# Splitting each gathered expert row into a U transfer and a V transfer, in a mixture-of-experts block fused with a sparse-attention block (Trainium2, one core)

## The chip, the cores and the metric

The kernel runs on one core of one Trainium2 chip. The metric is device time in microseconds (us) of one execution; three runs of the kernel before are shown by their median. One further execution was profiled, and every row below comes from that one.

## The reference, cut to what matters

The program computes two transformer blocks over 16 meta tokens and 256 real tokens of 1024 float32 features. The change lies in the feed-forward part of the first block, a retrieval of single-neuron experts. For each token, 8 heads choose 16 experts each out of 16,384, so 128 experts; for each chosen expert a row of U and a row of V, 1024 floats each, are read:

```python
def block(args):
    xt, e, g = args
    act = jax.nn.gelu(jnp.einsum('nkd,nd->nk', expert_u[e], xt), approximate=False)
    return jnp.einsum('nk,nkd->nd', g * act, expert_v[e])
```

The dot product of the token with the U row goes through a GELU and is scaled by the gate; the V rows are summed with these coefficients.

## The kernel before, in words

**Stages.** The kernel runs its stages one after the other. Most of them multiply activations by weights that SyncE streams from memory in 198 blocks of 512 KB through a ring of four buffers (`ring`, L364), each split into a high and a low part by ScalarE (L297) and VectorE (L305) and used by TensorE (L472). Between `w_peer_q` of the first block and the second block's first norm lies the expert stage, and during it the weight stream stands still.

**The expert stage.** 256 real tokens make two groups of 128, one token per partition. There are 8 heads by 2 token groups, 16 chains of 16 experts, so `SLOTS` = 256 slots. A slot is one expert for each of 128 tokens. For slot n:

- GpSimd (POOL) issues one indirect DMA (L424) that gathers 128 rows of `ROW` = 2048 floats. In the table a U row and its V row lie behind each other, so a row is 8 KB and a slot 1 MB. It goes into one of `ROWS` = 8 buffers of `gathered`. From slot 8 on POOL first waits for `row_used`, which says that slot n-8 has left its buffer (L423). At each sixteenth slot it also waits for `experts_chosen` (L421).
- VectorE waits for `row_landed` (L1463) and multiplies the U half with the token, summing (`dot`, L1469). It signals `dotted`. Between the dots it runs one or two steps of the selection of experts for the chain after next (`route_step`, L1391 to L1448).
- ScalarE waits for `dotted` (L1001), makes the GELU (L1002), the coefficient (L1005) and a diagonal matrix of the coefficients in one of `DIAGS` = 4 buffers (L1009), and signals `diag_ready`. Once per chain, for the first 14, it also makes an exponential between two loads of an activation table (L1029, L1031).
- TensorE waits for `diag_ready` (L687) and multiplies the diagonal with the V half in two matmuls of 512 columns (`add_row`, L689), each of which the profile shows as two. The last one signals `row_used`.

All engines take the slots in order. After 128 slots, and again after 256, ScalarE takes the sums (L1018) and TensorE transposes them (L698); VectorE adds them to the residual (L1489, L1512).

**What sets the order around the change.** Each engine's list of instructions is written out by hand, and semaphores alone tie them together. POOL does nothing else in this stage than issue gathers, one behind the other. A wait in front of one gather holds back all gathers behind it.

The lines that the change touches, beside those that the program prints here: the semaphores `row_landed` (L268), the host's table `rows` (L1716), which joins `expert_u` and `expert_v` along the columns, and the call of `build` (L1725).

Of the kernel before, what the change touches and what calls it, by code (L numbers as in the profile page):

```python
# [25 lines left out]
D = 1024  # L26
# [17 lines left out]
ROW = 2 * D  # L44
ROWS = 8
# [58 lines left out]
BANKS = 4  # L104


def build(nc, stream, rows_dram, small_dram, keys_dram, kiwi_dram, x_dram, out_dram):
    with ExitStack() as ctx:
        def sb(name, shape, dt=F32):
            return ctx.enter_context(nc.sbuf_tensor(name, shape, dt))  # L110

        def sem(name):
            return ctx.enter_context(nc.semaphore(name))
# [10 lines left out]
        small = sb("small", [P, SMALL_COLS])  # L124
# [71 lines left out]
        gathered = work[:, 0:ROWS * ROW].rearrange("p (r n) -> p r n", r=ROWS)  # L196
        base = ROWS * ROW
        route = {}
        for name, n in (("qp", PH * REAL), ("sc", CHAINS * 2 * NKEYS), ("v", 2 * TOPK), ("cand", SPREAD),
# [11 lines left out]
        expert = route["expert"].bitcast(U32)  # L211
# [53 lines left out]
        key_scores_ready, key_scores_taken, tops_shifted, tops_exp, experts_chosen, gates_ready = (  # L265
            sem(n) for n in ("key_scores_ready", "key_scores_taken", "tops_shifted", "tops_exp",
                             "experts_chosen", "gates_ready"))
        row_landed = [sem(f"row_landed{i}") for i in range(ROWS)]  # L268
        row_used, dotted, diag_ready, x_turned = (
            sem(n) for n in ("row_used", "dotted", "diag_ready", "x_turned"))  # L270
        y_summed, y_taken, y_turned, y_ready = (
# [61 lines left out]
        def tile_is_taken(eng, g):  # L333
            eng.wait_ge(tile_taken[g % BANKS], g // BANKS + 1)
# [40 lines left out]
        @block.gpsimd  # L375
        def _(pool):
            g = nc.gpsimd
            for tile, value in ((ones[:, :], 1.0), (eps[:, :], EPS), (one["ones_t"], 1.0), (zeros[:, :], 0.0), (ident[:, :], 0.0),
                                (one["tri"], 1.0), (one["rep"], 0.0), (one["bdtri"], 1.0), (one["win"], 0.0),
                                (one["blk64"], 1.0), (one["hide"], 0.0), (one["keep"], 1.0),  # L380
                                (one["bdm"], 1.0), (one["kbd"], 0.0)):
                g.memset(tile, value).then_inc(zeroed, 1)
            pool.wait_ge(zeroed, 14)
            g.iota(iota[:, :], [[1, NKEYS]], base=0, channel_multiplier=0,
                   allow_small_or_imprecise_dtypes=True).then_inc(consts, 1)
            g.affine_select(out=ident[:, :], in_=ident[:, :], compare_op=ALU.not_equal, fill=1.0, base=0,
                            pattern=[[-1, P]], channel_multiplier=1).then_inc(consts, 1)

            g.affine_select(out=one["tri"], in_=one["tri"], compare_op=ALU.is_ge, fill=0.0, base=0,
                            pattern=[[-1, P]], channel_multiplier=1).then_inc(consts, 1)  # L390

            v = one["rep"][0:META, :].rearrange("p (h m) -> p h m", m=META)
            g.affine_select(out=v, in_=v, compare_op=ALU.not_equal, fill=1.0, base=0,
                            pattern=[[0, P // META], [-1, META]], channel_multiplier=1).then_inc(consts, 1)

            g.memset(one["win"][:, P - META:P], 1.0).then_inc(consts, 1)

            for name, fill, off in (("keep", 0.0, 0), ("hide", NEG, -1)):
                for at, n in ((0, 2 * P), (2 * P, P)):
                    v = one[name][:, at:at + n]  # L400
                    g.affine_select(out=v, in_=v, compare_op=ALU.is_ge, fill=fill, base=off,
                                    pattern=[[1, n]], channel_multiplier=-1).then_inc(consts, 1)

            for n, (name, groups, size, inner) in enumerate((("bdtri", 8, META, META), ("blk64", 2, 64, 64),
                                                             ("bdm", 8, META, 64))):
                v = one[name].rearrange("p (g n) -> p g n", g=groups)
                g.affine_select(out=v, in_=v, compare_op=ALU.is_ge, fill=0.0, base=size - 1,
                                pattern=[[size, groups], [0, inner]],
                                channel_multiplier=-1).then_inc(pool_step, 1)
                pool.wait_ge(pool_step, n + 1)  # L410

                g.affine_select(out=v, in_=v, compare_op=ALU.is_ge, fill=0.0, base=0,
                                pattern=[[-size, groups], [-1 if name == "bdtri" else 0, inner]],
                                channel_multiplier=1).then_inc(consts, 1)

            pool.wait_ge(d_ready, 9)
            g.memset(qbd_flat, 0.0).then_inc(qbd_zeroed, 1)

            for n in range(SLOTS):
                if n % TOPK == 0:  # L420
                    pool.wait_ge(experts_chosen, n // TOPK + 1)  # L421
                if n >= ROWS:
                    pool.wait_ge(row_used, n - ROWS + 1)  # L423
                g.indirect_dma_start(  # L424
                    out=gathered[:, n % ROWS, :], out_offset=None, in_=rows_dram,
                    in_offset=bass.IndirectOffsetOnAxis(ap=expert[:, n:n + 1], axis=0)
                ).then_inc(row_landed[n % ROWS], 16)

            pool.wait_ge(y_ready, 1)
            g.memset(two["vis"], 0.0).then_inc(pool_step, 1)  # L430
            pool.wait_ge(pool_step, 4)
            g.affine_select(out=two["vis"], in_=two["vis"], compare_op=ALU.is_ge, fill=NEG, base=META,
                            pattern=[[-1, META + P]], channel_multiplier=1).then_inc(vis_ready, 1)

            pool.wait_ge(sigmoid_ready, 1)
            for n in range(C):
                tile_is_taken(pool, TILE0["w_conv_out_2"] + n)
                g.tensor_tensor(yco[:, n, :], yco[:, n, :], feat2[:, GB + n, META:],  # L438
                                ALU.mult).then_inc(conv_gated, 1)
# [6 lines left out]
        def _(pe):  # L446
# [168 lines left out]
            for i in range(SUBS):  # L615
                for j in range(2):
                    n = 2 * i + j
# [66 lines left out]
            def add_row(n):  # L684

                t, k = n // (SLOTS // 2), n % (SLOTS // 2)
                pe.wait_ge(diag_ready, n + 1)  # L687
                for j in range(2):
                    last = mm(ps[:, Y_BANK[t] + j, :], diag[:, n % DIAGS, :],  # L689
                              gathered[:, n % ROWS, D + 512 * j:D + 512 * j + 512],  # L690
                              start=k == 0, stop=k == SLOTS // 2 - 1)
                last.then_inc(row_used, 1)
# [10 lines left out]
            for n in range(SLOTS):  # L703
                add_row(n)
                if n == SLOTS // 2 + 4:
                    turn_sums(0, y_turned)
# [42 lines left out]
            for n in range(16):  # L749
# [9 lines left out]
                rows = slice(64 * (h % 2), 64 * (h % 2) + 64)  # L759
# [406 lines left out]
        def _(dve):  # L1166
            v = nc.vector
# [72 lines left out]
            for h in range(8):  # L1240
                rows = slice(64 * (h % 2), 64 * (h % 2) + 64)
                i = v.tensor_copy(kbd[rows, h // 2, META * h:META * h + META], feat[rows, 4 + h // 2, 0:META])
# [71 lines left out]
            for e in range(2):  # L1314
                rows = slice(64 * e, 64 * e + 64)
# [4 lines left out]
            for n in range(2 * SUBS):  # L1320
                i, j = n // 2, n % 2
# [10 lines left out]
            for j in range(2):  # L1332
                for cols, bank, at in ((slice(0, 2 * P), 4 + j, 0), (slice(2 * P, W), 6, 256 * j)):
                    n = cols.stop - cols.start
# [9 lines left out]
            for h in range(4):  # L1344
                i = stt(mix[:, 4 + h, :], ps[:, h // 2, 256 * (h % 2):256 * (h % 2) + 256],
                        small[:, at + h:at + h + 1], sil[:, h, :], ALU.mult, ALU.mult)
# [113 lines left out]
            def dot(n):  # L1460

                t = n // (SLOTS // 2)
                dve.wait_ge(row_landed[n % ROWS], 16 * (n // ROWS + 1))  # L1463
                if n % (SLOTS // 2) == 0:
                    dve.wait_ge(x_turned, t + 1)
                if n >= 2:
                    dve.wait_ge(dotted, n - 1)
                bank = (6, 0)[t]
                v.tensor_tensor_reduce(  # L1469
                    R["product"][:, D * (n % 2):D * (n % 2) + D], gathered[:, n % ROWS, 0:D],  # L1470
                    ps[:, bank:bank + 2, :].rearrange("p b n -> p (b n)"), 1.0, 0.0, ALU.mult, ALU.add,
                    R["dot"][:, n:n + 1]).then_inc(dotted, 1)
# [56 lines left out]
            for t in range(2):  # L1529
                seen = META + P * (t + 1)  # L1530
                for h in range(IDX_HEADS):
                    n = 8 * t + h
# [3 lines left out]
                    out = score[:, t, 0:seen] if h == 0 else rel[:, n % 2, 0:seen]  # L1536
# [25 lines left out]
            u = feat2[:, CU:CU + 8, :]  # L1562
            for c in range(C):
# [10 lines left out]
                i = tt(yc[:, c, :], yc[:, c, :], feat2[:, CB + c, META:], ALU.mult)  # L1574
# [36 lines left out]
            for n in range(8):  # L1611
                ahead(FIRST["w_attn_out_2"] + n)
                g = TILE0["w_attn_out_2"] + n
# [6 lines left out]
                i = tt(ya[:, n, :], yc[:, n, :], yco[:, n, :], ALU.add)  # L1620
# [7 lines left out]
            with dve.Fori(0, FF // 2) as i:  # L1628
                for k in range(RING):
                    ahead(b0 + k, i)  # L1630
                    if k > 1:
                        g = g0 + k
# [96 lines left out]
```

## Time and profile before

| what | value |
|---|---|
| median of 3 runs | 1484.89 us (1483.54 to 1484.93) |
| profiled execution, its own time | 1484.9 us |
| its span, from the first to the last instruction | 1482.9 us |
| outside the span | 2.0 us |
| mean granted TensorE clock | 0.959 of full speed |
| busy: TensorE, VectorE, ScalarE, GpSimd | 85%, 60%, 43%, 18% of the span |
| the chain that ended last, by engine | TensorE 54%, DMA 32% (gathers alone 31%), VectorE 5%, ScalarE 4%, issue 4% |
| gathers: queue, packets, bytes | software_dynamic, 36,864 packets, 268.45 MB |

How to read it: a busy share is an average over stages with different limits. The profile also cuts the span into 40 slices of 37.07 us; the expert stage fills the slices 8 to 24. "DMA" there is the mean busy share of the core's 16 DMA engines and "GB/s" what they moved. The chain that ended last is followed back from the last instruction through what released each step. "Idle before" is how long an engine stood still in front of an instruction, and the name behind the arrow is what ended that wait.

### The profile page before, as it was taken

What the parts mean: (1) busy time and instruction counts of PE and PEld (TensorE: products, weight loads), DVE (VectorE), ACT (ScalarE), POOL (GpSimd) and SP (SyncE); (2) the same over time, 40 slices, a digit from 0 to 9 for tenths busy, and PEclk for the clock granted to TensorE, in tenths of its full rate; (3) what the DMA queues carried; (4) which work ended last, traced back from release to release, by engine and by line L of the source; (5) the groups of instructions that cost most, each with busy time, mean ns of one, the idle gap of its engine ahead of it and who ended that gap; (6) DMA issues with size and microseconds to landing.
All of it is one profiled execution on the core that took longest, in us unless ns stands there. A gap on an engine that the chain in (4) does not pass through costs nothing.

```text
span 1482.9 us, 19506 instructions
## 1 busy us (share of the span) xinstructions
PE 1265.6 (85%) x6686; PEld 893.4 (60%) x6686; DVE 882.4 (60%) x1844; ACT 640.3 (43%) x1395; POOL 262.9 (18%) x300
## 2 busy tenths in 40 slices
PE   5999989677778777777787775899999989899996
PEld 5987778222222222222222222899999989899996
DVE  5445256766666666666666545476835556644455
ACT  4464244344444444444344434334434563533443
POOL 3000000433333333333333330000000020000000
PEclk9999588899999999999999998899999999999998
DMA  5420033999999999999999993245544345455551
GB/s 208 156 86 29 0 114 117 415 420 422 421 422 421 421 421 421 422 421 421 421 406 421 421 420 124 86 143 174 171 139 130 111 134 171 139 185 182 174 182 68
DMA packets 66743, 376.72 MB, mean 254 GB/s; under 512 B 7408, under 2 KB 7408, under 8 KB 33904
## 3 DMA queue, kind: packets, MB, share of 16 engines
q0 software_dynamic: 36864, 268.45, 43.6%
q1 hardware_dynamic: 29664, 106.81, 22.0%
q8 instruction: 38, 0.62, 0.2%
q10 hardware_dynamic: 144, 0.56, 0.1%
q14 instruction: 33, 0.27, 0.0%
HBM read 374.74 MB, written 1.05 MB: 253 GB/s over the span
## 4 chain that ended last, share of the span: by engine, by line
PE 54%; DMA 32%; DVE 5%; ACT 4%; issue 4%; DVEq 0%; SPq 0%; ACTq 0%
PE ps L472 32%; DMA work<-in_rows,work 31%; PE ps L689 6%; PE ps L723 4%; PE ps L507 1%; PE ps L510 1%; PE ps L513 1%; ACT work L1009 1%; PE ps L621 1%; DVE work L1197 1%; DVE work L1469 1%; ACT work L1005 1%; DVE work L1183 1%; DVE work L1202 1%; PE ps L625 1%
## 5 line engine op out<-in xcount | busy, mean ns | idle before, releaser
L689 PE MATMUL ps<-work 128*128 128x512 f32 x1024 | 507.4, 624 | 143.9 <-ACT work L1009 143.6
L689 PEld LDWEIGHTS ps<-work 128*128 128x128 f32 x1024 | 178.4, 192 | 471.5 <-ACT work L1009 324.2
L1469 DVE CUSTOM_DVE_ANT_0 work<-work,ps 128x1024 f32<-128x1024 f32 x256 | 312.7, 1221 | 225.7 <-DMA work<-in_rows,work 225.7
L472 PE MATMUL ps<-x_hi,w_hi 128*128 128x256 f32 (+1 forms) x1280 | 325.8, 295 | 24.2 <-ACT x_hi L315 17.1
L305 DVE TENSOR_TENSOR w_lo<-ring,w_hi 128x1024 fp32r<-128x1024 f32 x198 | 242.6, 1230 | 163.9 <-ACT w_hi L297 162.6
L424 POOL DMA_INDIRECT work<-in_rows,work x256 | 240.1, 938 | 525.7 <-PE ps L689 389.1
L472 PE MATMUL ps<-x_lo,w_hi 128*128 128x256 f32 (+1 forms) x1280 | 316.2, 288 | 0.0
L472 PEld LDWEIGHTS ps<-x_hi,w_hi 128*128 128x128 f32 x1280 | 244.3, 195 | 33.4 <-issue 27.2
L472 PEld LDWEIGHTS ps<-x_lo,w_hi 128*128 128x128 f32 x1280 | 242.4, 193 | 0.3
L297 ACT ACTIVATE w_hi<-ring 128x1024 fp32r<-128x1024 f32 x198 | 204.7, 1052 | 60.3 <-PE ps L723 28.6
L1002 ACT ACTIVATE work<-work 128x1 f32<-128x1 f32 x256 | 51.9, 203 | 357.3 <-DVE work L1469 355.8
L472 PE MATMUL ps<-x_hi,w_lo 128*128 128x256 f32 (+1 forms) x1280 | 186.7, 289 | 0.0
L472 PEld LDWEIGHTS ps<-x_hi,w_lo 128*128 128x128 f32 x1280 | 171.8, 195 | 0.0
L865 ACT ACTIVATE work<-ps 128x272 f32<-128x272 f32 (+2 forms) x96 | 37.7, 393 | 192.2 <-PE ps L472 159.5
L1009 ACT ACTIVATE work<-ident,work 128x128 f32<-128x128 f32 x256 | 102.7, 401 | 8.4
L1005 ACT ACTIVATE work<-work 128x1 f32<-128x1 f32 x256 | 75.4, 294 | 8.3
L438 POOL TENSOR_TENSOR work<-work 128x256 f32<-128x256 f32 x8 | 8.6, 1104 | 294.2 <-ACT work L1113 290.1
L507 PE MATMUL ps<-w_hi,x_hi 128*128 128x256 f32 x192 | 55.2, 287 | 0.0
L513 PE MATMUL ps<-w_hi,x_lo 128*128 128x256 f32 x192 | 53.9, 281 | 0.0
L510 PE MATMUL ps<-w_lo,x_hi 128*128 128x256 f32 x192 | 53.9, 281 | 0.0
L507 PEld LDWEIGHTS ps<-w_hi,x_hi 128*128 128x128 f32 x192 | 36.1, 188 | 1.3 <-issue 0.4
L1140 ACT ACTIVATE work<-ps 128x256 f32<-128x256 f32 x22 | 8.4, 383 | 64.6 <-PE ps L472 64.6
(236 smaller groups left out, 1084.5 us busy)
## 6 DMA issues: line engine op xcount, KB each, us to landing
ring<-in_stream SPq DMA_DIRECT2D x198, 512.0 KB, 3.4
work<-in_rows,work POOLq DMA_INDIRECT x256, 15.3
res<-in_tokens SPq DMA_DIRECT2D x4, 272.0 KB, 3.5
out_dram<-work SPq DMA_DIRECT2D x2, 512.0 KB, 2.8
work<-in_kiwi ACTq DMA_DIRECT2D x1, 544.0 KB, 3.3
work<-in_keys SPq DMA_DIRECT2D x1, 512.0 KB, 9.0
small<-in_small SPq DMA_DIRECT2D x1, 297.0 KB, 5.1
```

The source lines that it names most:

```text
L297: nc.scalar.activation(w_hi[:, k, :], ring[:, k, :], ACT.Copy).then_inc(w_hi_ready, 1)
L305: nc.vector.tensor_tensor(w_lo[:, k, :], ring[:, k, :], w_hi[:, k, :].bitcast(F32), ALU.subtract).then_inc(w_lo_ready, 1)
L424: g.indirect_dma_start(out=gathered[:, n % ROWS, :], out_offset=None, in_=rows_dram, in_offset=bass.IndirectOffsetOnAxis(ap=expert[:, n:n ...
L472: last = mm(out, w[:, k, c * P:(c + 1) * P], x[:, c, :], start=n == 0, stop=n == 3 * C - 1)
L507: i = mm(out, xh[:, c, at:at + P], hi, start=c == 0, stop=False)
L510: i = mm(out, xh[:, c, at:at + P], lo, start=False, stop=False)
L513: last = mm(out, xl[:, c, at:at + P], hi, start=False, stop=c == C - 1)
L689: last = mm(ps[:, Y_BANK[t] + j, :], diag[:, n % DIAGS, :], gathered[:, n % ROWS, D + 512 * j:D + 512 * j + 512], start=k == 0, stop=k == ...
L723: i = mm(ps[:, 4 + m // 2, 256 * (m % 2):256 * (m % 2) + 256], w[:, k, m * P:(m + 1) * P], x, start=False, stop=True, skip_group_check=True)
L1005: link(a(route["coef"][:, n:n + 1], route["gelu"][:, n:n + 1], ACT.Copy, scale=route["gate"][:, n:n + 1]))
L1009: a(diag[:, n % DIAGS, :], ident[:, :], ACT.Copy, scale=route["coef"][:, n:n + 1]).then_inc(diag_ready, 1)
L1469: v.tensor_tensor_reduce(R["product"][:, D * (n % 2):D * (n % 2) + D], gathered[:, n % ROWS, 0:D], ps[:, bank:bank + 2, :].rearrange("p b ...
```

## The change

Each slot's gather becomes two. The table of joined rows becomes two tables, `u` and `v`, of 4 KB rows. For each slot POOL issues a gather of 128 U rows (512 KB) into the first half of the slot's buffer and a gather of 128 V rows into the second half. From slot 8 on the U gather waits for `dotted` of slot n-8 and the V gather for `row_used` of slot n-8. VectorE's dot waits for the U half alone; TensorE gets a wait of its own for the V half. The buffers, their number and all arithmetic stay as they are.

```diff
-        row_landed = [sem(f"row_landed{i}") for i in range(ROWS)]
+        u_landed = [sem(f"u_landed{i}") for i in range(ROWS)]
+        v_landed = [sem(f"v_landed{i}") for i in range(ROWS)]
...
             for n in range(SLOTS):
                 if n % TOPK == 0:
                     pool.wait_ge(experts_chosen, n // TOPK + 1)
+                offset = bass.IndirectOffsetOnAxis(ap=expert[:, n:n + 1], axis=0)
+                if n >= ROWS:
+                    pool.wait_ge(dotted, n - ROWS + 1)
+                g.indirect_dma_start(out=gathered[:, n % ROWS, 0:D], out_offset=None, in_=u_dram,
+                                     in_offset=offset).then_inc(u_landed[n % ROWS], 16)
                 if n >= ROWS:
                     pool.wait_ge(row_used, n - ROWS + 1)
-                g.indirect_dma_start(
-                    out=gathered[:, n % ROWS, :], out_offset=None, in_=rows_dram,
-                    in_offset=bass.IndirectOffsetOnAxis(ap=expert[:, n:n + 1], axis=0)
-                ).then_inc(row_landed[n % ROWS], 16)
+                g.indirect_dma_start(out=gathered[:, n % ROWS, D:ROW], out_offset=None, in_=v_dram,
+                                     in_offset=offset).then_inc(v_landed[n % ROWS], 16)
...
             def add_row(n):
                 t, k = n // (SLOTS // 2), n % (SLOTS // 2)
+                pe.wait_ge(v_landed[n % ROWS], 16 * (n // ROWS + 1))
                 pe.wait_ge(diag_ready, n + 1)
...
             def dot(n):
                 t = n // (SLOTS // 2)
-                dve.wait_ge(row_landed[n % ROWS], 16 * (n // ROWS + 1))
+                dve.wait_ge(u_landed[n % ROWS], 16 * (n // ROWS + 1))
...
-    arrays = {"stream": stream, "rows": np.concatenate([a["expert_u"][0], a["expert_v"][0]], axis=1), "small": np.ascontiguousarray(small),
+    arrays = {"stream": stream, "u": a["expert_u"][0], "v": a["expert_v"][0], "small": np.ascontiguousarray(small),
```

## Rows read from the trace of the kernel before

**Rows 1.** Stretches: busy us (instructions) of each engine, granted clock, DMA share, GB/s.
```profile
core 0: us, PE busy (x) PEld busy (x) DVE busy (x) ACT busy (x) POOL busy (x), PEclk, DMA share, GB/s
8.20:11.70 3.50, 1.25 (x2) 0.50 (x2) 3.36 (x5) 1.96 (x4) 3.43 (x4) 1.00 1.02 416
270.00:570.00 300.00, 238.03 (x481) 84.55 (x480) 199.16 (x543) 127.31 (x386) 112.36 (x120) 0.98 1.01 421
...
745.00:755.00 10.00, 9.86 (x19) 4.31 (x20) 7.46 (x25) 3.68 (x13) 3.57 (x4) 0.83 0.95 369
755.00:895.00 140.00, 109.63 (x223) 37.57 (x222) 80.12 (x185) 56.06 (x176) 51.71 (x56) 1.00 1.01 421
895.00:900.00 5.00, 4.00 (x9) 1.39 (x9) 2.52 (x5) 1.80 (x6) 0.00 (x0) 1.00 0.76 315
902.00:906.00 4.00, 3.33 (x7) 1.35 (x8) 2.38 (x4) 1.03 (x4) 0.00 (x0) 1.00 0.06 27
```

**Rows 2.** Who waited for whom, us 257 to 912: total us, times, longest.
```profile
POOL work L424 <- PE ps L689: 389.1, 246, 5.5
...
DVE work L1469 <- DMA work<-in_rows,work: 225.7, 252, 2.2
```

**Rows 3.** The gathers of L424: duration in ns, and from issue to landing.
```profile
L424 POOL DMA_INDIRECT work<-in_rows,work x256: 933/936/1124, 257.0 to 892.0; - x128
...
DMA to landing us min/median/max: 6.4/15.3/16.3
```

**Rows 4.** DMA in us 8.2 to 11.7, weights and keys, no gather: packets and queue.
```profile
DMA packets 401, 1.45 MB, mean 416 GB/s; under 512 B 46, under 2 KB 46, under 8 KB 401
...
q1 hardware_dynamic: 401, 1.45, 101.9%
```

**Rows 5.** DMA in us 270 to 570, inside the expert stage: packets and queue.
```profile
DMA packets 17349, 126.41 MB, mean 421 GB/s; under 512 B 1923, under 2 KB 1923, under 8 KB 1923
...
q0 software_dynamic: 17335, 126.26, 101.2%
```

**Rows 6.** DMA in us 257 to 912: instruction fetches; on the page, those of the span.
```profile
q8 instruction: 8, 0.13, 0.1%
...
span 1482.9 us, 19506 instructions
...
q8 instruction: 38, 0.62, 0.2%
```

**Rows 7.** POOL in order of time, us 256 to 276: start, duration, idle before.
```profile
256.98 1.12 POOL L424 DMA_INDIRECT work<-in_rows,work  x1 [129.78 <-DVE work L1447]
258.41 0.94 POOL L424 DMA_INDIRECT work<-in_rows,work  x1 [0.30 <-issue]
259.65 0.94 POOL L424 DMA_INDIRECT work<-in_rows,work  x1 [0.31 <-issue]
...
264.62 0.94 POOL L424 DMA_INDIRECT work<-in_rows,work  x1 [0.30 <-issue]
265.87 0.93 POOL L424 DMA_INDIRECT work<-in_rows,work  x1 [0.31 <-issue]
```

**Rows 8.** POOL around two of its gathers with a wait, close together.
```profile
585.78 0.94 POOL L424 DMA_INDIRECT work<-in_rows,work  x1 [3.28 <-PE ps L689]
587.17 0.94 POOL L424 DMA_INDIRECT work<-in_rows,work  x1 [0.46 <-PE ps L689]
```

**Rows 9.** POOL around one of ScalarE's exponentials, us 497 to 514.
```profile
501.06 0.94 POOL L424 DMA_INDIRECT work<-in_rows,work  x1 [2.51 <-PE ps L689]
506.37 0.94 POOL L424 DMA_INDIRECT work<-in_rows,work  x1 [4.38 <-PE ps L689]
```

**Rows 10.** The last slot and what follows it, in order of time.
```profile
907.30 1.22 DVE L1469 CUSTOM_DVE_ANT_0 work<-work,ps 128x1024 f32<-128x1024 f32 x1 [1.23 <-DMA work<-in_rows,work]
...
909.58 1.98 PE L689 MATMUL ps<-work 128*128 128x512 f32 x4 [0.48 <-ACT work L1009]
911.61 1.09 ACT L1018 ACTIVATE work<-ps 128x512 f32<-128x512 f32 x2 [2.07 <-PE ps L689]
```

More of the change, by code:

```diff
@@ L104, with build @@
 BANKS = 4
-def build(nc, stream, rows_dram, small_dram, keys_dram, kiwi_dram, x_dram, out_dram):
+def build(nc, stream, u_dram, v_dram, small_dram, keys_dram, kiwi_dram, x_dram, out_dram):
     with ExitStack() as ctx:
@@ L1724 @@
     out = nc.dram_tensor("out_dram", (P, C * REAL), F32, kind="ExternalOutput").ap()
-    build(nc, dram["stream"], dram["rows"], dram["small"], dram["keys"], dram["kiwi"], dram["tokens"], out)
+    build(nc, dram["stream"], dram["u"], dram["v"], dram["small"], dram["keys"], dram["kiwi"], dram["tokens"], out)
     r = run_bass_kernel_spmd(nc, [{f"in_{k}": v for k, v in arrays.items()}], core_ids=[0])
```

## The prediction

> **What bounds the kernel now.** I began with the table of stretches. From 270 to 570 us and from 755 to 895 us the core's 16 DMA engines are busy all the time (share 1.01) and move 421 GB/s [rows 1]. So the expert stage runs at the pace of its transfers: a slot is 1,048,576 bytes, at 421 GB/s 2.49 us, and 256 slots are 638 us of the 650 us between the first gather and the last dot [rows 7, 10]. The second view, who waited for whom, confirms it from the consumer's side: VectorE waited for gathered rows 252 times out of 256, 225.7 us in all, while POOL waited 389.1 us for TensorE to give buffers back [rows 2]. POOL's wait looks like a lack of buffers, but a gather takes 15.3 us from its issue to its landing and only 6.4 us where nothing is queued ahead of it [rows 3]. Most of a buffer's life is spent in the DMA queue. A buffer that comes free sooner makes that queue longer and moves no byte sooner.
>
> The third view is the end of the stage. From 902 to 906 us the DMA share is 0.06, one engine of sixteen, at 27 GB/s [rows 1]. The others are through at about 899 (0.76 of the 5 us from 895 on). One DMA engine is some 7 us behind the rest, every slot waits for its part, and its work sets the stage's length. Instruction fetches fit as the cause: 8 in this stage, 0.1% of 16 engines over 655 us, so up to 1.3 us each [rows 6].
>
> **The change part by part.** The sum is made against the profiled execution's own time, 1484.9 us (span 1482.9 and 2.0 outside); the median of the runs is the same to 0.1 us. From no change a measurement of this kernel can tell about 0.2%, 3 us.
>
> *The DMA engines.* 128 packets of 8 KB and 16 completion packets per slot become 256 of 4 KB and 32. The trace has no gather of 4 KB rows. The nearest row is the start of the kernel, where 512 KB blocks with 4 KB per partition fill the engines as fully (share 1.02): 416 GB/s, against 421 for the gathers [rows 1]. A slot at 416 GB/s is 2.521 us instead of 2.491, 0.030 us more, times 256 = 7.7 us. The upper bound comes from the time that packets take. At the start 16 engines times 3.5 us times 101.9% is 57.1 us for 355 data packets, 0.161 us each with their completions [rows 4]. In the gathers it is 16 x 300 x 101.2% = 4858 us for 15,412, 0.315 each [rows 5]. Two small ones are 0.006 us longer than one large one; an engine has 8 such pairs per slot, 0.05 us, times 256 = 13 us. The lower bound is nothing: I exclude a gain, as no row shows 4 KB packets faster than the gathers. I take 7.7, since it is a rate of whole transfers at a full load and the upper bound counts the overlap of packets twice.
>
> [...]
>
> *POOL.* 256 more gathers of 0.94 us. Unhindered, issues follow each other in 1.24 us, 0.30 of it between two instructions (259.65 to 265.87, five intervals) [rows 7]. Two per slot are 2.49 us, which is all of a slot's time. Today POOL is busy half of it. 511 intervals from 257.2 put the last V gather at 892.4 us; today's last is issued at 892.0 [rows 3]. So POOL alone doesn't lengthen the stage, and at 2.52 us per slot it keeps 0.03 us spare: cost 0. What it loses is the power to catch up. Around ScalarE's exponential TensorE is late, and POOL stands still for 4.38 us in place of some 1.5 [rows 9]; fourteen chains have that. A lag of 3 us then stays for many slots. It is covered by the queue: 15.3 less 6.4 is 9 us of work ahead of each gather. Once POOL lags, its waits are already met and further stalls pass it by.
>
> *The waits on POOL.* U of slot n waits for `dotted` of n-8, V for `row_used` of n-8. `dotted` comes earlier: the dot starts 2.28 us before TensorE, and TensorE takes 1.98 more [rows 10]. But U of n stands behind V of n-1 in POOL's list, and that waits for `row_used` of n-9. The U half can thus start about one issue (1.24 us) earlier than now, and no more. It lengthens a queue that is already long: 0.
>
> *VectorE and TensorE.* A dot needs only the U half, which the slowest engine delivers half a slot, 1.25 us, before the V half. In the stage this moves the dots forward without making the engine faster. At the end it counts: today 2.28 us lie between the last landing and TensorE's start on it [rows 10]; with U landing 1.25 us earlier 1.03 us are left. Gain 1.25. TensorE's new wait is for a V half that lands within 1.25 us of the U half, while the coefficient takes 2.28: met when it is reached, and TensorE works 2 us of 2.49. At the start the first dot waits for VectorE's routing, not for rows: 0.
>
> *Instruction fetches.* About 256 gathers and 256 waits of TensorE are added to a program that fetches 38 packets for 19,506 instructions, 513 per packet [rows 6]: one more, about 1 us if it hits the slowest engine. I take 1.
>
> Sum: +7.7 - 1.25 + 1 = +7.4, so 1492.3 us.
>
> **The rivals.** *No change to tell.* The 416 of the start is a stretch of 3.5 us only. If the engines are limited by bytes and the small packets cost under 0.012 us per slot (3 us in all), the tail's gain and the cost cancel: 1484.9 - 1.25 + 0 to 3 = 1484 to 1487. Against it: the number of completion packets doubles for certain.
>
> *Faster.* The U half no longer waits for `row_used`, dots run 1.25 us ahead, and the one hole in the transfers, 369 instead of 421 GB/s from 745 to 755 [rows 1], closes. That hole is 10 x (1 - 369/421) = 1.2 us. With the tail's 1.25 it makes 2.5, and with free packets 1482.4 us; over 0.2% needs a little more than the trace holds. This is the other side of my forecast, and it decides only where 4 KB packets cost nothing.
>
> *POOL becomes the bound.* All intervals of 1.24 us are between gathers without a wait. The shortest between two with a wait is 1.39 (585.78 to 587.17), and there TensorE released the second [rows 8]. So an interval with a wait that is already met lies between 1.24 and 1.39. After the last V issue come at least 6.4 less half a slot, 5.2, to the landing, and 2.0 of TensorE. At 1.24 that ends at 899.6, today TensorE ends at 911.6 [rows 10], with my forecast at 919: POOL decides above 1.28 us. At 1.31 the end is 933.8, +22; at 1.39 the last issue is at 967.5 and the end at 974.7, +63, so 1548. Also, up to 16 transfers would be in flight where 8 are now, and nothing shows what POOL does with so many. For it: 512 issues without a margin. Against: 256 gathers of 0.936 us in the median, the longest 1.124 [rows 3], beside a busy VectorE.
>
> *The slow engine falls further behind.* If its lag comes from reading the gathers' descriptors rather than from fetches, twice as many descriptors double the 7 us: 1492.3 + 7 = 1499. [...]
>
> *The change doesn't do what it says.* Separate release of the halves is mostly undone by POOL's fixed order, as worked out above. I hold this for certain, and it is in the forecast.
>
> **How the numbers follow.** The forecast (packets cost 5 to 13 us) has 0.45; the slow engine 0.10; POOL as the bound 0.17; no change 0.20; faster 0.08. Slower by over 0.2% is the first three, 0.72. The time is the forecast's, 1492.3. Its own range is 1488 (5 us for packets) to 1499 (13 us and two fetches). The range reaches down to 1484, the no-change case, and up to 1506, POOL with an interval of 1.31 us. Left out are the faster case and the upper part of POOL's, together under 0.2.
>
> **What would show it.** Right: in the expert stage a DMA share of 1.0 and about 416 GB/s; 512 gathers of 0.94 us; VectorE still waiting for U rows nearly each slot, about 0.6 to 1.2 us; POOL waiting only some tens of us in all; the last gather's landing near 914 us and TensorE's last matmul 3 us behind it. The POOL rival: issues at equal intervals above 1.28 us without waits, landings in 5 to 7 us, DMA share under 0.97. The slow engine: a stretch of 10 us or more at share 0.06 at the end. The forecast is wrong if the rate in the stage is 421 GB/s or more, or if the transfers have gaps while POOL never waits.

## The result, and the profile after

The changed kernel takes 1504.96 us (median of 4 runs, 1504.11 to 1505.45); the kernel before took 1484.91 beside it. The ratio is 1.0136, 95% interval 1.0120 to 1.0152: slower by 20 us. The forecast was 1492.3 with a range up to 1506.0. The direction and the engine were right; the size was 2.7 times the 7.4 us that I had summed. Of the six runs with gathers of 64 rows, further down, four were slow (1888 to 2033 us), so the median of the two others stands there, though the profile is of a slow one.

The profiled execution spans 1502.1 us, 19.2 more than before. First the page: engines, queues and DMA issues of the changed kernel.

```profile
PE 1265.0 (84%) x6686; PEld 896.8 (60%) x6686; DVE 882.7 (59%) x1844; ACT 640.2 (43%) x1395; POOL 503.9 (34%) x556
...
q0 software_dynamic: 73728, 268.47, 44.9%
...
work<-in_u,work POOLq DMA_INDIRECT x256, 16.0
work<-in_v,work POOLq DMA_INDIRECT x256, 16.0
```

The same bytes come in twice the packets (73,728 for 36,864). POOL is busy nearly twice as long (503.9 us for 262.9), VectorE, ScalarE and TensorE as long as before. Then the stretches, which answer to [rows 1]; the columns are busy us (instructions) of each engine, granted clock, DMA share and GB/s.

```profile
8.20:11.70 3.50, 1.25 (x2) 0.50 (x2) 3.36 (x5) 1.82 (x4) 3.43 (x4) 1.00 1.02 411
270.00:570.00 300.00, 231.28 (x470) 83.31 (x469) 194.93 (x530) 124.42 (x377) 225.09 (x240) 0.98 1.03 409
...
745.00:755.00 10.00, 7.58 (x17) 2.71 (x16) 6.15 (x15) 4.92 (x15) 7.25 (x9) 1.00 1.03 410
755.00:895.00 140.00, 106.22 (x217) 37.50 (x216) 81.98 (x197) 55.63 (x172) 101.10 (x108) 0.99 1.03 409
...
915.00:920.00 5.00, 3.83 (x9) 1.35 (x8) 2.44 (x5) 1.80 (x6) 0.00 (x0) 1.00 0.37 150
920.00:925.00 5.00, 3.92 (x9) 1.35 (x8) 2.45 (x5) 1.79 (x6) 0.00 (x0) 1.00 0.08 29
```

The engines are full (1.03) and yet move only 409 GB/s for the whole stage, where they moved 421. A slot is 1,048,576 bytes: 2.564 us in place of 2.491. The difference of 0.073 us times 256 is 18.7 us, nearly all of the loss. Look at the first row too: the stretch on which the forecast's main term stood, the same code in both kernels, reads 411 here and read 416 before.

The waits from 270 to 910 us (total us, times, longest) show who is held up by whom, as [rows 2] did.

```profile
DVE work L1474 <- DMA work<-in_u,work: 234.8, 245, 2.3
...
POOL work L430 <- issue: 69.2, 217, 0.4
POOL work L426 <- issue: 65.0, 213, 0.4
POOL work L430 <- PE ps L694: 23.4, 34, 3.0
```

VectorE still waits for rows at almost every slot. POOL is hardly held up by TensorE any more (23.4 us); what stands between its gathers is the 0.30 us between two instructions. The end of the stage, in order of time, answers to [rows 10]:

```profile
924.37 1.22 DVE L1474 CUSTOM_DVE_ANT_0 work<-work,ps 128x1024 f32<-128x1024 f32 x1 [1.27 <-DMA work<-in_u,work]
...
926.74 1.95 PE L694 MATMUL ps<-work 128*128 128x512 f32 x4 [0.55 <-ACT work L1014]
928.73 1.09 ACT L1023 ACTIVATE work<-ps 128x512 f32<-128x512 f32 x2 [2.14 <-PE ps L694]
```

TensorE ends at 928.7 us against 911.6: 17.1 us later. The remaining 2.1 us of the span lie behind the stage, in code that the change doesn't touch. Stretches of 100 us there, with the whole remainder last; the kernel before:

```profile
911.60:1482.90 571.30, 530.03 (x4146) 513.86 (x4146) 328.54 (x493) 252.54 (x387) 9.15 (x10) 0.96 0.44 143
```

and the changed kernel:

```profile
928.70:1502.10 573.40, 532.15 (x4146) 516.00 (x4146) 328.38 (x493) 252.46 (x387) 9.14 (x10) 0.96 0.43 142
1178.70:1278.70 100.00, 94.01 (x725) 90.14 (x725) 57.06 (x81) 52.02 (x77) 8.62 (x8) 0.98 0.43 139
1278.70:1378.70 100.00, 93.32 (x751) 92.60 (x751) 53.35 (x58) 42.34 (x53) 0.00 (x0) 0.95 0.51 167
```

The same 4146 matmuls take 2.1 us longer. In the second and third rows the granted clock averages 0.98 and 0.95; before, the two stretches at the same distance from the stage's end (1161.6 to 1261.6 and 1261.6 to 1361.6) had 1.00 and 0.97, so TensorE's granted clock was a little lower here. The same remainder, from TensorE's end in the expert stage to the end of the span, took 571 to 575 us in the profiles of all versions below but the one with 64 rows, and 575.3 in one that differs from the kernel before in its last slot alone. So the 2.1 us are within what this part varies by.

### The profile page after: what moved, and what is told of

It is laid out like the page before. It is cut to its first block, busy times and chain, and to the rows that moved or that the text cites. A ratio compares the mean times of both kernels' runs of the same rounds, so it can differ in the third digit from the quotient of the medians.

```text
span 1502.1 us, 20017 instructions
## 1 busy us (share of the span) xinstructions
PE 1265.0 (84%) x6686; PEld 896.8 (60%) x6686; DVE 882.7 (59%) x1844; ACT 640.2 (43%) x1395; POOL 503.9 (34%) x556
## 3 DMA queue, kind: packets, MB, share of 16 engines
q0 software_dynamic: 73728, 268.47, 44.9%
## 4 chain that ended last, share of the span: by engine, by line
PE 51%; DMA 19%; POOL 13%; issue 7%; ACT 5%; DVE 4%; DVEq 0%; SPq 0%; ACTq 0%
PE ps L476 31%; DMA work<-in_u,work 19%; POOL work L430 7%; POOL work L426 6%; PE ps L728 4%; PE ps L694 3%; PE ps L511 1%; PE ps L514 1%; PE ps L517 1%; PE ps L625 1%; DVE work L1202 1%; ACT L1036 1%; ACT L1034 1%; ACT work L1014 1%; DVE work L1188 1%
## 5 line engine op out<-in xcount | busy, mean ns | idle before, releaser
L476 PE MATMUL ps<-x_hi,w_hi 128*128 128x256 f32 (+1 forms) x1280 | 326.4, 296 | 24.2 <-ACT x_hi L316 17.1
L426 POOL DMA_INDIRECT work<-in_u,work x256 | 240.7, 940 | 207.6 <-DVE work L1452 129.7
L430 POOL DMA_INDIRECT work<-in_v,work x256 | 240.3, 939 | 94.1 <-issue 70.8
```

Of the source, the lines that this page charges most:

```text
L426: g.indirect_dma_start(out=gathered[:, n % ROWS, 0:D], out_offset=None, in_=u_dram, in_offset=offset).then_inc(u_landed[n % ROWS], 16)
L430: g.indirect_dma_start(out=gathered[:, n % ROWS, D:ROW], out_offset=None, in_=v_dram, in_offset=offset).then_inc(v_landed[n % ROWS], 16)
L476: last = mm(out, w[:, k, c * P:(c + 1) * P], x[:, c, :], start=n == 0, stop=n == 3 * C - 1)
```

## The experiments

Three theories. *Packets:* the DMA engines pay for each data packet, so 4 KB rows are slower than 8 KB rows whoever issues or waits. *Transfers:* what costs is the second transfer of a slot, with its completion packets, what has to be prepared for it, and its issue. *Release:* the new waits or POOL's full list hold the transfers up. Times are medians; GB/s are those of 270 to 570 us. The figures in square brackets are 95% intervals of the ratio to the kernel before, which ran beside each version.

**Both halves released and awaited together.** The split alone, without the separate release.

```diff
-                    pool.wait_ge(dotted, n - ROWS + 1)
+                    pool.wait_ge(row_used, n - ROWS + 1)
                 g.indirect_dma_start(out=gathered[:, n % ROWS, 0:D], ...)
-                if n >= ROWS:
-                    pool.wait_ge(row_used, n - ROWS + 1)
...
                 dve.wait_ge(u_landed[n % ROWS], 16 * (n // ROWS + 1))
+                dve.wait_ge(v_landed[n % ROWS], 16 * (n // ROWS + 1))
```

> The changed kernel, still with two gathers per slot, but both halves of a buffer are released together (the U gather waits for row_used too, the V gather for nothing of its own) and VectorE waits for both halves before a dot. Packet theory (the DMA engines pay for each packet of 4 KB, whoever waits for what): nothing changes but the end, 1504 to 1507 us, 409 GB/s in the stage. Release theory (the cost lies in the new waits or in POOL being held up between two halves): most of the 20 us come back, 1485 to 1492 us.

Measured: 1505.11 us (1503.78 to 1506.63), ratio to before 1.0134 [1.0114, 1.0154].

```profile
270.00:570.00 300.00, 227.22 (x467) 80.96 (x466) 193.44 (x523) 123.59 (x374) 222.38 (x238) 0.99 1.03 409
```

The release theory falls: with the old rule of release the loss is the same. In the medians of the runs, releasing and awaiting each half by itself neither costs nor brings anything. In the traces it brings the little that was forecast for the end: from the first gather to TensorE's last matmul this version takes 673.7 us (254.7 to 928.4) and the changed kernel 671.9 (256.8 to 928.7).

**Two gathers of 64 rows of 8 KB.** Meant to double the transfers and leave the data packets as they are.

```diff
-                g.indirect_dma_start(
-                    out=gathered[:, n % ROWS, :], out_offset=None, in_=rows_dram,
-                    in_offset=bass.IndirectOffsetOnAxis(ap=expert[:, n:n + 1], axis=0)
-                ).then_inc(row_landed[n % ROWS], 16)
+                for part in range(2):
+                    g.indirect_dma_start(
+                        out=gathered[64 * part:64 * part + 64, n % ROWS, :], out_offset=None, in_=rows_dram,
+                        in_offset=bass.IndirectOffsetOnAxis(ap=expert[0:64, n:n + 1], axis=0)
+                    ).then_inc(half_landed[part][n % ROWS], 16)
...
-                dve.wait_ge(row_landed[n % ROWS], 16 * (n // ROWS + 1))
+                for part in range(2):
+                    dve.wait_ge(half_landed[part][n % ROWS], 16 * (n // ROWS + 1))
```

> The kernel before with two gathers per slot, each of 64 rows of 8 KB, issued and released together. Data packets stay 128 of 8 KB per slot, transfers and completion packets double. The partitions 64 to 127 get the rows of the tokens 0 to 63, so their sums are of other experts. Packet theory, with the 0.072 us per slot spread evenly over 8 more data packets and 1 more completion packet per engine, 0.008 us each: only the completion is left, +2 us, 1487 us, about 419 GB/s. Transfer theory (what costs is a transfer: its issue, its descriptors, its completion): all of the stage's 17 us, 1502 us, 409 GB/s.

Measured: 1857.41 us (1851.61 and 1863.19), ratio 1.2507 [1.2465, 1.2549]. Neither theory had this.

```profile
DMA packets 10360, 67.91 MB, mean 226 GB/s; under 512 B 2073, under 2 KB 2073, under 8 KB 2073
...
q0 software_dynamic: 10354, 67.85, 101.5%
```

The engines are as full as before (101.5% for 101.2%), but a packet of 8 KB takes 16 x 300 x 101.5% / 8281 = 0.588 us, against 0.315 before [rows 5]. Each transfer writes to 64 neighbouring partitions of the 128, and the stage moves 226 GB/s in place of 421. That the number of partitions sets the rate is my estimate from these two rates; no run varied the partitions otherwise. The two gathers of a slot also read the same 64 rows, and no run tells whether that cost something. As a test of transfers against packets it failed, since it changed something larger.

**Rows of 16 KB, one gather for two slots.** The packet theory in the other direction.

```diff
+                if n % 2:
+                    continue
                 if n >= ROWS:
-                    pool.wait_ge(row_used, n - ROWS + 1)
+                    pool.wait_ge(row_used, n - ROWS + 2)
                 g.indirect_dma_start(
-                    out=gathered[:, n % ROWS, :], out_offset=None, in_=rows_dram,
+                    out=work[:, ROW * (n % ROWS):ROW * (n % ROWS + 2)], out_offset=None, in_=rows_dram,
...
-                dve.wait_ge(row_landed[n % ROWS], 16 * (n // ROWS + 1))
+                dve.wait_ge(row_landed[n % ROWS // 2 * 2], 16 * (n // ROWS + 1))
...
-"rows": np.concatenate([a["expert_u"][0], a["expert_v"][0]], axis=1)
+"rows": np.concatenate([a["expert_u"][0], a["expert_v"][0]] * 2, axis=1)
```

> The kernel before with one gather of 128 rows of 16 KB for two slots; both slots compute with the expert of the even one. Per slot and engine 4 data packets of 16 KB in place of 8 of 8 KB, and half a completion. Packet theory with 0.008 us per packet: 4.5 fewer, 0.036 us per slot, -9 us, 1476 us, about 427 GB/s. If the rate is capped by bytes above 8 KB packets: 1484 to 1486 us and 421 GB/s. If releasing buffers in pairs starves the engines: DMA share under 0.98 and a time above 1487 us.

Measured: 1478.12 us (1476.83 to 1480.70), ratio 0.9953 [0.9938, 0.9968], 7 us faster. The page's rates in 40 slices:

```profile
GB/s 209 157 86 30 0 115 107 419 428 422 428 427 406 413 429 427 422 415 428 427 409 428 427 424 126 89 155 171 171 144 128 110 134 171 139 186 180 173 182 65
```

The undisturbed slices of the stage stand at 427 to 429, as foretold; others fall to 406, and so the mean is 423. POOL's longest wait for a pair of buffers between 270 and 570 us is 13.4 us, which makes the release in pairs the likely cause of the falls; it wasn't tested by itself. The three sizes are now in line: a slot takes 2.450 us at 428 GB/s, 2.491 at 421 and 2.564 at 409. That is 0.041 us for 4 more packets per engine, then 0.073 for 8 more: 0.009 to 0.010 us each.

**Half the bytes.** What can POOL do by itself?

```diff
-                g.indirect_dma_start(out=gathered[:, n % ROWS, 0:D], ...)
+                g.indirect_dma_start(out=gathered[:, n % ROWS, 0:D // 2], ...)
...
-                g.indirect_dma_start(out=gathered[:, n % ROWS, D:ROW], ...)
+                g.indirect_dma_start(out=gathered[:, n % ROWS, D:D + D // 2], ...)
```

The tables have rows of 512 floats, the dot reads 512 features and both matmuls read `D:D + 512`.

> The changed kernel with half the bytes of every U and V row: 512 gathers of 128 rows of 2 KB; the dot runs over 512 features and both matmuls use the same 512 columns. The DMA engines need at most 1.4 us per slot, TensorE 1.7, so POOL's issues alone set the pace. If a wait that is already met costs POOL nothing, issues follow each other in 1.24 us also from slot 8 on, 2.49 us per slot, last issue near 893 us, TensorE's end near 899 us, total about 1472 us. If a met wait costs up to 0.15 us (intervals of 1.39 us), 2.79 us per slot and about 1548 us. Only in the first case had the changed kernel's POOL 0.07 us per slot to spare.

Measured: 1476.88 us (1475.70 to 1480.01), ratio 0.9942 [0.9923, 0.9961]. POOL in order of time, and its V gathers:

```profile
299.82 0.95 POOL L426 DMA_INDIRECT work<-in_u,work  x1 [0.30 <-issue]
301.07 0.94 POOL L430 DMA_INDIRECT work<-in_v,work  x1 [0.30 <-issue]
302.32 0.95 POOL L426 DMA_INDIRECT work<-in_u,work  x1 [0.30 <-issue]
```

```profile
L430 POOL DMA_INDIRECT work<-in_v,work x256: 942/946/958, 258.6 to 896.7; - x128
...
DMA to landing us min/median/max: 3.4/3.7/4.5
```

With waits that are already met the interval is 1.25 us, against 1.24 without waits [rows 7]. POOL's own pace is 2.50 us per slot, and here it is the bound: gathers land 3.7 us after their issue, so nothing is queued. The time is 5 us above the 1472 expected, of which the 0.01 us per issue explains most (the last V gather is issued at 896.7 in place of 893), and far below the 1548 of costly waits. At half the bytes the kernel gains no more than 8 us. In the changed kernel POOL had 0.06 us per slot to spare.

**Plain loads from POOL, 8 KB and 4 KB rows.** 128 consecutive rows in place of chosen ones, so the sums are of other experts; the same holds for all versions with plain loads below.

```diff
-                g.indirect_dma_start(
-                    out=gathered[:, n % ROWS, :], out_offset=None, in_=rows_dram,
-                    in_offset=bass.IndirectOffsetOnAxis(ap=expert[:, n:n + 1], axis=0)
-                ).then_inc(row_landed[n % ROWS], 16)
+                g.dma_start(gathered[:, n % ROWS, :], rows_dram[P * (n % 128):P * (n % 128) + P, :]
+                            ).then_inc(row_landed[n % ROWS], 16)
```

The 4 KB version does the same with both transfers of the changed kernel.

> The kernel before, but POOL issues a plain load of 128 consecutive rows of the joined table in place of the gather (other experts, so other sums). Same queue, same 8 KB packets, consecutive addresses. If random rows cost nothing in memory: 421 GB/s and 1483 to 1486 us. If the gathers lose time to scattered rows: up to 427 GB/s, 1475 us.

> The changed kernel with plain loads of 128 consecutive rows of 4 KB, U and V apart, issued by POOL. Packet theory: the rate is that of 4 KB packets whatever the addresses, 409 GB/s, and the time is 17 to 20 us above the kernel with plain loads of 8 KB. If scattered 4 KB rows are what costs: no more than 5 us above it, and 416 GB/s or more. POOL's time per plain load is not known; if it is over 1.28 us, POOL is the bound and the DMA share tells so.

Measured: 1486.35 us (ratio 1.0014 [1.0004, 1.0025]) and 1503.32 us (1.0126 [1.0109, 1.0144]), 17.0 us apart. The 8 KB version:

```profile
270.00:570.00 300.00, 239.01 (x481) 85.05 (x480) 198.50 (x540) 127.65 (x387) 63.82 (x121) 0.98 1.01 421
```

The 4 KB version:

```profile
270.00:570.00 300.00, 228.61 (x469) 81.40 (x467) 193.90 (x530) 124.65 (x378) 123.62 (x234) 0.99 1.03 409
```

These are the rates of the gathers, 421 and 409. Scattered rows cost no rate against consecutive ones, at either size. A plain load also keeps POOL busy for 0.53 us (123.62 / 234) in place of 0.94, so POOL had plenty to spare and the loss was nearly the same.

**The same loads from SyncE's hardware queue.** SyncE's loop over the weight blocks is cut after block 43 and the loads of the 256 slots stand between, with the waits of the kernel before (8 KB) or of the changed one (4 KB).

```diff
-            with sp.Fori(1, BLOCKS // RING) as i:
+            with sp.Fori(1, 11) as i:
...
+            for n in range(SLOTS):
...
+                sp.dma_start(gathered[:, n % ROWS, :], rows_dram[P * (n % 128):P * (n % 128) + P, :]).then_inc(row_landed[n % ROWS], 16)
+            with sp.Fori(11, BLOCKS // RING) as i:
```

> The kernel before with the loads of 128 consecutive 8 KB rows issued by SyncE in its hardware queue, with the same waits; POOL issues none. If the software queue and its descriptors cost nothing: as the plain loads from POOL, 421 GB/s. If they cost: above 421 GB/s and below 1484 us.

> The same with 4 KB rows of U and V apart, by SyncE, with the waits of the changed kernel. It tells what the 416 GB/s at the start of the kernel before was worth, which is this kind of transfer over 3.5 us. If a hardware queue really moves 4 KB packets at 416: 2.52 us per slot, 1490 to 1493 us, 7 to 8 above the 8 KB version, and the rest of the 17 us belongs to the software queue. If 416 was an accident of a short window: 409 to 411 GB/s and 15 to 20 us above the 8 KB version.

Measured: 1483.32 us (ratio 0.9998 [0.9987, 1.0008]) and 1500.51 us (1.0107 [1.0090, 1.0124]), 17.2 us apart, at 421 and at 409 GB/s. The stretch at the start and the one in the stage, of the 4 KB version:

```profile
8.20:11.70 3.50, 1.24 (x2) 0.50 (x2) 3.40 (x4) 1.94 (x4) 3.36 (x5) 1.00 1.02 414
270.00:570.00 300.00, 227.46 (x469) 80.98 (x468) 193.88 (x527) 124.66 (x377) 0.00 (x0) 0.99 1.03 409
```

Both rows are the same queue and the same packet size, once over 3.5 us and once over 300. The short one lies 5 GB/s above the long one. That is no accident of a short window: over the 13 profiles of this study the stretch at the start reads 405 to 420, in the mean 416 and in twelve of them 411 or more, while the 80 stretches of 3.5 us from 270 to 550 us of this version read 403 to 412. The start really moves its 4 KB packets faster than the stage does, and it isn't the queue or the packet size that makes the difference, since both are the same here.

**One transfer of 4 KB runs, and one of two slots.** Transfers and packets pulled apart at last, with plain loads from POOL. The first takes U and V of a slot from two tables in one transfer:

```diff
-                g.dma_start(gathered[:, n % ROWS, :], rows_dram[P * (n % 128):P * (n % 128) + P, :]
+                g.dma_start(gathered[:, n % ROWS, :].rearrange("p (h n) -> p h n", h=2),
+                            uv_dram[:, P * (n % 128):P * (n % 128) + P, :].rearrange("h p n -> p h n")
```

> The kernel with plain loads from POOL, one transfer per slot as before, but of two runs of 4 KB per partition (U and V tables apart): 4 KB packets with one transfer's 16 completion packets and the waits of the kernel before. Packet-size theory (the 0.072 us per slot come with the 4 KB data packets): 409 to 411 GB/s, 1500 to 1504 us. Transfer theory (they come with the second transfer, its completions or its issue): 421 GB/s, 1483 to 1487 us.

The second loads two slots in one transfer, with the waits of the 16 KB rows:

```diff
+                g.dma_start(work[:, ROW * (n % ROWS):ROW * (n % ROWS + 2)].rearrange("p (h n) -> p h n", h=2),
+                            rows_dram[P * (n % 128):P * (n % 128) + 2 * P, :].rearrange("(h p) n -> p h n", h=2)
```

> Plain loads from POOL, one transfer for two slots, of two runs of 8 KB per partition: 8 KB packets, half the transfers and half the completion packets, buffers released in pairs. Packet-size theory: as one transfer per slot, 421 GB/s, 1484 to 1487 us. Transfer theory, by which half a transfer less per slot saves half of 0.072 us: 427 GB/s, 1476 us. Read beside the 16 KB rows, which gave 423 GB/s.

Measured: 1506.32 us (1502.43 to 1507.89, ratio 1.0134 [1.0114, 1.0153]) and 1489.25 us (1485.09 to 1491.18, 1.0028 [1.0015, 1.0040]). DMA of the first, from 270 to 570 us:

```profile
DMA packets 31814, 122.74 MB, mean 409 GB/s; under 512 B 1868, under 2 KB 1868, under 8 KB 31801
```

and of the plain loads with two transfers per slot:

```profile
DMA packets 33686, 122.76 MB, mean 409 GB/s; under 512 B 3743, under 2 KB 3743, under 8 KB 33671
```

The completion packets are halved (1868 for 3743), the data packets are equal, and the rate is 409 in both. The transfer theory falls: the second transfer, its completions and its issue change nothing in the rate. The rates of the second kernel in slices:

```profile
GB/s 208 156 86 29 1 114 133 423 421 422 420 420 407 413 422 421 420 419 412 409 411 422 422 421 124 87 155 171 170 148 120 114 128 163 136 185 182 173 183 68
```

Its good slices are at 421 or 422, not at 427: fewer transfers with the same packets gain nothing. It has falls to 407 and 413 as the 16 KB rows have, and shares with them the one transfer for two slots and the paired release. Both times are some 2 us above the top of what the packet theory had given (1504 and 1487); in both profiles the part behind the stage took 575 us, the upper end of what it takes anywhere.

**The last slot alone split.** The gain at the end by itself.

```diff
+                if n < SLOTS - 1:
                     g.indirect_dma_start(out=gathered[:, n % ROWS, :], ..., in_=rows_dram, ...).then_inc(row_landed[n % ROWS], 16)
+                else:
+                    g.indirect_dma_start(out=gathered[:, n % ROWS, 0:D], ..., in_=u_dram, ...).then_inc(row_landed[n % ROWS], 16)
+                    g.indirect_dma_start(out=gathered[:, n % ROWS, D:ROW], ..., in_=v_dram, ...).then_inc(v_landed, 16)
```

> The kernel before, with the last slot alone split into a U gather and a V gather. The tail term by itself: the last dot starts half a slot earlier, TensorE starts about 1.1 us after the last landing in place of 2.3 and ends near 910.4 us in place of 911.6, total 1483.7 us; in the median of the runs hardly to be told from 1484.9. If the tail's gain was none, TensorE ends at 911.6 us or later.

Measured: 1485.95 us (12 runs, 1482.35 to 1488.07), ratio 1.0003 [0.9993, 1.0014]: no difference.

```profile
904.53 1.22 DVE L1477 CUSTOM_DVE_ANT_0 work<-work,ps 128x1024 f32<-128x1024 f32 x1
...
905.56 3.70 PE L697 MATMUL ps<-work 128*128 128x512 f32 x8 [0.49 <-ACT work L1017]
```

The last dot starts with no wait in front of it, right behind the one before. TensorE then finds two slots together (8 matmuls in one piece) and ends at 909.3, 4.7 us after the start of the last dot, 4.3 before. It ends 2.3 us earlier than before, but its first gather was also 1.3 us earlier (255.7 for 257.0), which leaves 1.0. From the landing of the last V half (issued at 891.7, landed 14.0 us later) to TensorE's end are 3.5 us, where the whole row took 4.3: the split gains 0.8 us there, less than 1.2, since TensorE still has the slot before in hand. Behind the stage this execution loses that again: 575.3 us from 909.3 to its end, against 571.3. No version that computes the same sums is faster than the kernel before; the 16 KB rows are, but two experts that a token chooses don't lie side by side.

## Why the prediction was right or wrong

**What bounds the stage: right.** The DMA engines' share stayed at 1.0 and more, VectorE waited for rows at 251 of 256 slots, and loads from three kinds of issue gave one rate for one packet size: gathers, plain loads from POOL and loads from SyncE moved 421 GB/s in rows of 8 KB and 409 in rows of 4 KB.

**The term for the DMA engines: the step that failed, in its size.** I put +7.7 us, taking the 416 GB/s at the start of the kernel for the rate of 4 KB rows in the stage, and 13 us as the upper bound. It is 409 GB/s, 0.073 us per slot, +18.7. The mechanism was the one named, a price per packet, and the experiments confirm it against both rivals: between 4 and 16 KB the difference comes to 0.009 to 0.010 us per packet of an engine. In every run with full engines a packet is one row, so whether the price belongs to the packet or to the piece of memory that it reads stays open.

What was wrong was the step from one stretch to the other. 416 was not an unlucky reading: it is the mean of that stretch over the 13 profiles. In the changed kernel, 78 of the 80 stretches of 3.5 us from 270 to 550 us read 403 to 412 (the first two 387 and 419). So the start moves the same size of packet some 7 GB/s faster, and that hid 7 of the 12 GB/s that I had to forecast. Neither the queue nor the packet size does it, as the loads from SyncE show; which of the other differences does, what is read, how much is in flight or what the other engines do meanwhile, no run shows. The bound from packet durations came from the same 3.5 us, so it was no second witness: it gave 0.161 us per 4 KB packet, where the changed kernel has 16 x 300 x 102.5% / 29,925 = 0.164, from the two rows of its DMA between 270 and 570 us:

```profile
DMA packets 33681, 122.74 MB, mean 409 GB/s; under 512 B 3741, under 2 KB 3741, under 8 KB 33666
...
q0 software_dynamic: 33666, 122.59, 102.5%
```

With 0.1644 the same working gives (2 x 0.1644 - 0.3152) x 8 = 0.109 us per slot, 28 us in all. Durations do overstate, as I had said, since 18.7 was measured; but by this working the upper bound was 28 and not 13, and the forecast's own range, 1488 to 1499, was too narrow.

**POOL: right.** No cost. Its interval with met waits is 1.25 us, under the 1.28 from which it would decide, and the gathers' landing times tell that it runs ahead: their medians (U, changed kernel) grow from 6.8 us between 270 and 300 us to 14.6 between 450 and 500, and stay at 16.5 to 16.7 after that. That is 0.1 us per slot (7.8 us in some 74 slots) by which the DMA engines fell behind POOL, not the reverse; 0.06 to 0.07 of it is the mean rate (2.564 less 2.50), and the slowest engine's own lag fits as the rest. The loads from SyncE, with no work for POOL at all, gave the same 409 GB/s. That the time landed near the top of a range whose upper end was POOL's is chance, not support for that rival. (An interval of 1.31 us gives 1507 by my own sum, not the 1506 of the range.)

The landings of the U gathers, first from 270 to 300 us, then from 450 to 500:

```profile
DMA to landing us min/median/max: 6.4/6.8/7.2
...
DMA to landing us min/median/max: 13.9/14.6/16.2
```

**The slow engine: the rival fell.** At the end the mean of the engines is through at about 917 (0.37 of the 5 us from 915 on), the last U half lands at 924.3 and the V half at 925.6: 9 us of lag. The kernel before had 907.2 less 899, so 8. That reading the gathers' descriptors causes the lag was the rival's supposition; no row shows such reads. Twice the gathers, in twice the packets (73,728 for 36,864), didn't double it. And with the 8 KB loads in SyncE's hardware queue

```profile
895.00:900.00 5.00, 4.00 (x9) 1.35 (x8) 2.49 (x5) 1.80 (x6) 0.00 (x0) 1.00 0.59 240
```

the mean is through at 898.0 and the last dot starts at 903.9, a lag of 6 us; with the 4 KB loads there it is 7. Most of the lag is there without the gathers. What makes one engine slow stays open.

**The waits: right.** Holding back the separate release left the rate at 409 GB/s and the time within 0.2 us.

**The tail: right in the changed kernel, in the traces.** From the last dot's start to TensorE's is 2.37 us, and the V half lands half a slot, 1.3, after U, so 1.1 us are left of 2.3. From the last landing to TensorE's last matmul are 3.1 us; with both halves awaited together 4.5, and 4.3 in the kernel before. Gain 1.2. The medians of the runs are too coarse to show it (1504.96 and 1505.11). The stage ends 17.1 us later, which is 18.7 less 1.2 within half a microsecond.

**Instruction fetches:** one more on the page (39 for 38), as forecast; whether it cost its 1 us no run shows. The 2.1 us behind the stage were not in the sum; they go with a lower granted clock there, and the other profiles vary as much.

## What to carry to other kernels

Where the DMA engines are full, ask of every change what it does to the size of the packets: here splitting rows cost 0.009 us for each further packet of an engine, and releasing half of a buffer sooner brought no rate (409 GB/s with and without it). A rate borrowed from another stretch carries the difference between the two stretches, and this one came out again in profile after profile, so reading it more often would not have helped. When the term is a per cent, either measure the rate in the place where it will be used, by one small run with the new row size, or give the range the width of what rates at the same packet size differ by.

## What was not expected of the hardware

Two gathers for 64 neighbouring partitions each ran at 226 GB/s, where one of 128 ran at 421, with the DMA engines full in both cases. And rows of 2 KB didn't make packets of 2 KB. In the kernel with half the bytes the profile has, from 270 to 570 us:

```profile
DMA packets 19205, 63.05 MB, mean 210 GB/s; under 512 B 3839, under 2 KB 3839, under 8 KB 19190
...
q0 software_dynamic: 19190, 62.89, 73.8%
```

That is 62.89 MB in 19,190 - 3,839 = 15,351 data packets, 4.1 KB each: two rows to a packet. At rows of 4, 8 and 16 KB, every row was a packet of its own: 122.59 MB in 29,925 data packets, 126.26 in 15,412 and, with the 16 KB rows, 126.67 in 7,731, so 4.1, 8.2 and 16.4 KB each. A packet of two such rows takes 16 x 300 x 73.8% / 15,351 = 0.231 us, more than the 0.164 of one 4 KB row. The engines were not full in that run, so this is no price, but where rows are smaller, a count of packets is not a count of rows.
